# Strassen-type block sums in the output projections of a two-layer LRU and attention kernel, and an output bias added by DMA

## What is computed

```python
# layer 0                                            D_MODEL = D_RNN = 2048, SEQ = 256
return (jax.nn.gelu(gate_br) * rec) @ w_out + b_out      # (256 x 2048) @ (2048 x 2048) + row
# layer 1
return o.reshape(bsz, seq, N_HEADS * V_D) @ w_o          # (256 x 2048) @ (2048 x 2048)
# both layers
h = h + block(rmsnorm(h, norm_mix[layer]))
h = h + swiglu(rmsnorm(h, norm_ffn[layer]))
```

## Time and profile before

| | |
|---|---|
| median of 3 runs | 1996.56 us (1995.83 to 1996.84) |
| the profiled execution: its own time | 1996.43 us |
| its span in the profile | 1994.6 us |
| PE busy | 1974.2 us, 99%, 9907 matmuls |
| DVE busy | 1649.1 us, 83% |
| ACT busy | 1136.6 us, 57% |
| POOL busy | 76.5 us, 4% |
| loads of `lru_w_out`, `w_o` | 16 of 1 MB each |
| `project(0)` | 227.5 to 316 us of the span |
| `project(2)` | 1191 to 1289 us of the span |

### The profile page before, as it was taken

How to read it: one execution, slowest core, us unless ns; L and a number is a source line. 1 busy time by engine, 2 the same in 40 slices (tenths; PEclk the granted TensorE clock), 3 DMA queues, 4 the chain that set the end, 5 groups by cost and what they waited for, 6 DMA issues and landing times.

```text
span 1994.6 us, 26207 instructions
## 1 busy us (share of the span) xinstructions
PE 1974.2 (99%) x9907; PEld 1683.8 (84%) x9907; DVE 1649.1 (83%) x1849; ACT 1136.6 (57%) x1356; POOL 76.5 (4%) x113
## 2 busy tenths in 40 slices
PE   7999999999999999999999999999999999999999
PEld 7999988888888888888898888888888888888887
DVE  6868655788888889999976886468988898899897
ACT  5478445555555556556676664455555555556564
POOL 1140200000000000000001110000000000000000
PEclk9999999999999999999999999999999999999999
DMA  8564663556556565565565435355656556655554
GB/s 278 170 206 158 206 212 115 199 193 202 197 191 209 191 204 194 195 206 192 209 201 169 127 126 185 111 189 192 205 194 205 194 191 208 193 196 203 200 202 168
DMA packets 159488, 378.21 MB, mean 190 GB/s; under 512 B 6154, under 2 KB 10516, under 8 KB 159028
## 3 DMA queue, kind: packets, MB, share of 16 engines
q1 hardware_dynamic: 158960, 376.02, 56.4%
q0 software_dynamic: 272, 1.13, 0.2%
q10 hardware_dynamic: 180, 0.05, 0.0%
HBM read 375.08 MB, written 2.10 MB: 189 GB/s over the span
## 4 chain that ended last, share of the span: by engine, by line
PE 89%; issue 5%; DVE 2%; ACT 1%; DMA 1%; POOL 1%; POOLq 0%; SPq 0%; DVEq 0%; ACTq 0%
PE bank L1731 75%; PE bank L1912 10%; PE bank L1692 2%; PE bank L1724 1%; PE bank L1715 1%; DVE w_lo L1005 0%; POOL stats L1676 0%; DMA h<-in_x 0%; ACT w_hi L555 0%; DMA raw<-in_ffn_w_in 0%; DMA raw<-in_ffn_w_out 0%; PE bank L1894 0%; ACT gtmp L687 0%; ACT w_hi L618 0%; ACT w_lo L621 0%
## 5 line engine op out<-in xcount | busy, mean ns | idle before, releaser
L1731 PE MATMUL bank<-w_hi,act_hi 128*128 128x512 f32 x1840 | 720.2, 391 | 1.7 <-issue 1.5
L1731 PE MATMUL bank<-w_hi,act_lo 128*128 128x512 f32 x1840 | 716.4, 389 | 0.0
L555 ACT ACTIVATE w_hi<-raw 128x2048 fp32r<-128x2048 f32 (+2 forms) x271 | 509.8, 1884 | 331.6 <-DMA raw<-in_ffn_w_in 149.5
L1731 PE MATMUL bank<-raw_lo,act_hi 128*128 128x512 f32 x1584 | 616.4, 389 | 0.0
L1005 DVE TENSOR_TENSOR raw_lo<-raw,w_hi 128x2048 fp32r<-128x2048 f32 x176 | 401.8, 2288 | 112.6 <-ACT w_hi L555 110.5
L1731 PEld LDWEIGHTS bank<-w_hi,act_hi 128*128 128x128 f32 x1840 | 345.5, 188 | 74.9 <-issue 2.6
L1731 PEld LDWEIGHTS bank<-w_hi,act_lo 128*128 128x128 f32 x1840 | 345.4, 188 | 72.1
L1731 PEld LDWEIGHTS bank<-raw_lo,act_hi 128*128 128x128 f32 x1584 | 297.5, 188 | 60.5
L1005 DVE TENSOR_TENSOR w_lo<-raw,w_hi 128x2048 fp32r<-128x2048 f32 (+2 forms) x95 | 211.8, 2240 | 84.3 <-ACT w_hi L555 84.0
L1055 DVE TENSOR_TENSOR raw_lo<-raw,w_hi 128x2048 fp32r<-128x2048 f32 x88 | 201.0, 2284 | 0.0
L618 ACT ACTIVATE w_hi<-raw 128x1024 fp32r<-128x1024 f32 x88 | 93.0, 1057 | 130.0 <-DMA raw<-in_ffn_w_in 107.9
(11 more groups left out here) (230 smaller groups left out, 2440.5 us busy)
## 6 DMA issues: line engine op xcount, KB each, us to landing
raw<-in_ffn_w_in SPq DMA_DIRECT2D x176, 1024.0 KB, 5.3
raw<-in_ffn_w_out SPq DMA_DIRECT2D x88, 1024.0 KB, 4.9
raw<-in_lru_w_in SPq DMA_DIRECT2D x32, 1024.0 KB, 5.4
raw<-in_lru_w_out SPq DMA_DIRECT2D x16, 1024.0 KB, 5.4
raw<-in_w_o SPq DMA_DIRECT2D x16, 1024.0 KB, 5.0
raw<-in_w_ukv SPq DMA_DIRECT2D x8, 1024.0 KB, 5.4
raw<-in_w_uq SPq DMA_DIRECT2D x8, 768.0 KB, 4.5
raw<-in_w_dkv SPq DMA_DIRECT2D x8, 576.0 KB, 4.3
```

What stands on the lines that cost most here:

```text
L555: A.activation(flat_chunk(w_hi, s, size), flat_chunk(raw, s, size), ACT.Copy).then_inc(w_hi_done, 1)
L1731: i = T.matmul(bank[:, :], x_part, w_part, start=first and n == 0, stop=last and n == 2)
```

## The change

In both projections, units 4 and 5 of the first pass and units 1 and 3 of the second (9 and 11 of the 16) become units of seven block products. With them come their activation sums, a `p1_out`, a `shared_add` and a `shared_to_h` in each pass, which stand in iterations 5 and 11. All low parts of the projections' chunks go to `raw_lo`, so all loads from chunk 4 of a projection on, and the first four of the following `up`, wait for `chunk_used`. The second pass has as its own banks those that were shared in the first, and shares the first pass' own: unit 8 waits for the first `shared_add` (`u_done`), unit 9 for the first pass' `results_to_h` (`h_done`). The bias is added to `h` by two DMAs that POOL starts as soon as its last multiply of the gate stage is done.

The core of the diff, in the order SP, ACT, DVE, POOL, PE (the helpers of `two_pass` were split so that `project` can call them too, and numbers of semaphores shifted with them):

```diff
+PROJ_SUMS = ((4, 5), (1, 3))
...
-                    unit(0, u, slice(0, W), u >= 4)
+                    unit(0, u, slice(0, W), True)
...
-                         raw[n % 4].rearrange("p (k f) n -> p k (f n)", k=2), in_place)
+                         raw[n % 4].rearrange("p (k f) n -> p k (f n)", k=2), in_place or n >= 4)
...
+            def p1_out(d, half, n):
+                act.wait_ge(chunk_used, DOWN_C[d] + n + 1)
+                act.wait_ge(h_shared, 2 * d + half)
+                A.activation(gtmp[:, 0, :], shared_banks(d, half)[0][:, :], ACT.Copy).then_inc(p1_done, 1)
...
                         stationary(d, g, wo_slot(g) if d else act_slot(g))
+                    half, v = divmod(n, KT // 2)
+                    if v == PROJ_SUMS[half][-1]:
+                        p1_out(d, half, n)
...
-                    split((DOWN_C[d] + n + 4) // 4, n % 4)
+                    proj_split(d, n + 4)
...
             def project(d):
                 for n in range(KT - 4):
+                    half, v = divmod(n, KT // 2)
+                    if v == PROJ_SUMS[half][-1]:
+                        if half:
+                            dve.wait_ge(h_sq, NB * d + 2)
+                        shared_to_h(d, half)
                     if n in (1, 3) or n == d == 0:
                         g = (n + 3) // 2
                         stationary(g, wo_slot(g) if d else act_slot(g), DOWN_G0[d] + g + 1)
                     if n == KT // 2 - 1:
                         results_to_h(d, 0, KT // 2)
-                    split((DOWN_C[d] + n + 4) // 4, n % 4)
+                    if proj_sum_no(n + 4) is not None:
+                        proj_sums(d, n + 4)
+                    proj_split(d, n + 4)
...
-            pool.wait_ge(y_done, 4)
-            pool.dma_start(bout[:, :], a["lru_b_out"][0:1, :].broadcast_to([P, D])).then_inc(bout_in, 16)
-            pool.wait_ge(bout_in, 16)
             for t in range(NT):
-                i = G.tensor_tensor(h[:, t, :], h[:, t, :], bout[:, :], ALU.add)
-            i.then_inc(bout_added, 1)
+                pool.dma_start(h[:, t, :], a["lru_b_out"][0:1, :].broadcast_to([P, D]),
+                               accum_op=ALU.add).then_inc(bout_added, 16)
...
+                if v == 0 and half:
+                    pe.wait_ge(u_done, U_DONE * (d // 2) + 1)
                 pe.wait_ge(w_lo_done, DOWN_C[d] + n + 1)
+                no = proj_sum_no(n)
+                if no is not None:
+                    pe.wait_ge(g_sum_lo, A_SUMS * (d // 2) + no + 1)
+                    if n == KT // 2 + PROJ_SUMS[1][0]:
+                        pe.wait_ge(h_done, NB * d + 2)
+                    i = sum_unit(s, no % 2, no % 3, k0, result, shared_banks(d, half), v == PROJ_SUMS[half][0],
+                                 v == PROJ_SUMS[half][-1], tiles=DOWN_TILES)
```

More of the change, by code:

```diff
@@ L521, in down_unit_no, with proj_sum_no @@
         def down_unit_no(f, n):
-            return SUMS * f + 3 * S_BLOCKS + down_sum_no(n)
+            return SUMS * f + PROJ_ALL + 3 * S_BLOCKS + down_sum_no(n)
+        def proj_sum_no(n):
+            half, v = divmod(n, KT // 2)
+            return len(PROJ_SUMS[0]) * half + PROJ_SUMS[half].index(v) if v in PROJ_SUMS[half] else None
         def banks_of(odd):
@@ L532, in pass_banks, with shared_banks @@
             return banks if d % 2 else [banks[n] for n in (0, 2, 1, 3)]
+        def shared_banks(d, half):
+            return banks_of((half + d) % 2 == 1)[1]
         def sum_tiles(t, e):
@@ L640, in two_pass @@
                 c0 = DOWN_C[d]
-                def p1_out(n, half):
-                    act.wait_ge(chunk_used, c0 + n + 1)
-                    act.wait_ge(h_shared, 2 * f + half)
-                    A.activation(gtmp[:, 0, :], banks_of(half == 0)[1][0][:, :], ACT.Copy).then_inc(p1_done, 1)
                 for n in range(DOWN_UNITS - 4):
@@ L997, in _, with split @@
             V = nc.vector
-            def split(m, s, of_pair=False, to=w_lo):
+            def split(m, s, of_pair=False, to=None):
                 if isinstance(m, int) and 4 * m + s >= CHUNKS:
                     return
+                if to is None:
+                    n = 4 * m + s if isinstance(m, int) else 0
+                    to = raw_lo if C_LOUT <= n < C_DKV or n >= C_WO else w_lo
                 size = chunk_size(4 * m + s if isinstance(m, int) else s + (C_PAIR if of_pair else 0))
@@ L1089, in down_sums, with activation_sums_lo, proj_sums, proj_split @@
                 V.tensor_tensor(s_raw[:, j, 3, :], a12, s_raw[:, j, 1, :], ALU.add).then_inc(g_sum, 1)
+            def activation_sums_lo(o, j):
+                dve.wait_ge(g_sum_hi, o + 1)
+                V.tensor_tensor(s_lo[:, j, :, :], s_raw[:, j, :, :], s_hi[:, j, :, :].bitcast(F32),
+                                ALU.subtract).then_inc(g_sum_lo, 1)
+            def proj_sums(d, n):
+                no, half, v = proj_sum_no(n), n // (KT // 2), n % (KT // 2)
+                m, s = (DOWN_C[d] + n) // 4, n % 4
+                k0 = 2 * ((v + KT // 4 * half) % (KT // 2)) if d else 2 * v
+                source_ready(dve, d, k0 // 4)
+                dve.wait_ge(chunk_used, 4 * m + s - 3)
+                activation_sums(k0, A_SUMS * (d // 2) + no, no % 3)
+                sums(m, s, SUMS * (d // 2) + no, no % 2, DOWN_TILES)
+            def proj_split(d, n):
+                m, s, no = (DOWN_C[d] + n) // 4, n % 4, proj_sum_no(n)
+                if no is None:
+                    split(m, s)
+                else:
+                    activation_sums_lo(A_SUMS * (d // 2) + no, no % 3)
+                    split_sums(m, s, SUMS * (d // 2) + no, no % 2)
+            def down_sums(f, n):
+                d, g_no = 2 * f + 1, down_sum_no(n)
+                v, o, j = n % PASS_UNITS, A_SUMS * f + PROJ_ALL + g_no, g_no % 3
+                m, s = (DOWN_C[d] + n) // 4, n % 4
+                dve.wait_ge(gT_act, FB * f + v // 2 + 1)
+                dve.wait_ge(chunk_used, 4 * m + s - 3)
+                activation_sums(2 * v, o, j)
                 sums(m, s, down_unit_no(f, n), g_no % 2, DOWN_TILES)
@@ L1109, in results_to_h @@
                 result = pass_banks(d, half)
-                if d % 2:
-                    dve.wait_ge(h_shared, d + half)
-                elif d == 0 and half == 0:
-                    dve.wait_ge(bout_added, 1)
+                dve.wait_ge(h_shared, 2 * d + half + 1)
                 for b in (0, 1):
@@ L1142, in into_next, with shared_to_h @@
                     split((c_next + n) // 4, n, to=w_lo if d == 1 else raw_lo)
+            def shared_to_h(d, half):
+                f = d // 2
+                before = S_BLOCKS + 2 if d % 2 else 0
+                shared_add(shared_banks(d, half), SUM_BLOCKS * f + before + half,
+                           U_DONE * f + (FB + 2 if d % 2 else 0) + half)
+                if d == half == 0:
+                    dve.wait_ge(bout_added, 16 * NT)
+                for t in range(NT):
+                    hb = h[:, t, (2 * half) * W:(2 * half + 1) * W]
+                    V.tensor_tensor(hb, hb, gtmp[:, t, :], ALU.add)
+                for t in range(NT):
+                    hb = h[:, t, (2 * half + 1) * W:(2 * half + 2) * W]
+                    i = V.tensor_tensor(hb, hb, mix[:, t, :], ALU.subtract)
+                i.then_inc(h_shared, 1)
             def project(d):
                 for n in range(KT - 4):
+                    half, v = divmod(n, KT // 2)
+                    if v == PROJ_SUMS[half][-1]:
+                        if half:
+                            dve.wait_ge(h_sq, NB * d + 2)
+                        shared_to_h(d, half)
                     if n in (1, 3) or n == d == 0:
@@ L1756, in last_unit, with sum_unit @@
                 return i
-            def sum_unit(s, e, j, k0, result, shared, first, last, gT_needed, tiles=UP_TILES):
+            def sum_unit(s, e, j, k0, result, shared, first, last, gT_needed=None, tiles=UP_TILES):
                 own = [tuple(buf[s][:, n, :] for buf in (w_hi, raw_lo)) for n in tiles]
@@ L1768, in sum_unit @@
                 product(shared[3], s3, t3, first, last)
-                if first:
+                if first and gT_needed is not None:
                     pe.wait_ge(gT_act, gT_needed)
@@ L1812, in half_units @@
                         pe.wait_ge(w_lo_done, DOWN_C[d] + n + 1)
-                    i = plain_unit(n, tile_of(d, 0, n), pass_banks(d, 0), n == 0, False, tiles=DOWN_TILES, lo=w_lo, halves=(half,))
+                    i = plain_unit(n, tile_of(d, 0, n), pass_banks(d, 0), n == 0, False, tiles=DOWN_TILES, halves=(half,))
                     if half:
```

89 lines of the change are left out of this document (40 added, 49 removed).

## The result

The changed kernel takes **2010.35 us**, the median of 4 runs (2009.52 to 2012.46), against 1996.7 for the kernel before, run beside it: a ratio of 1.0070, 95% interval 1.0058 to 1.0082. It is slower by 13.7 us, within the range of the prediction and 4 us above its value. The profiled execution has a span of 2007.7 us, 13.1 more than before.

What follows compares the result with a forecast made beforehand. PE, busy 99%, sets the time if DVE delivers. Waits 14.8 plus restarts 0.5 less gain 5.44 is +9.9 us: span 2006.3, with 0.13 to the median 2006.4 us; own range 2003 to 2010, wider range 2000 to 2012.5.

Steps and rivals of the forecast that it cites:

- The gain: Both projections: eight units lose three matmuls each, 24 x 0.2268 = 5.44 us saved, 2.72 us per projection.
- The waits: Projections: PE waits for DVE at units 5 and 9, and at unit 4 of project(2), 14.8 us in all.
- Nothing for the bias and for the low parts in the slots: Bias by two accumulating DMAs, and later loads for the next up stage: each costs 0 us.
- Restart after a wait: After each of five PE waits, matmuls don't overlap with earlier ones: 0.1 us each, 0.5 us, bounds 0 and 0.39.
- The clock: Rival, chance 0.10: three PE waits of 3.35 to 5.5 us bring the clock down, 3 x 2.35 = 7 us, 2013.4.
- a cold array: Program start: matmuls 0.21 us apart, later 0.13, read as a possible slow state from 12.2 to 16.9.
- the helpers keep up: Rival, chance 0.10: DVE runs further ahead in the projections, waits shrink to nothing, only the 5.44 us saved is left, 1991.1.
- only unit 9 waits: Rival, chance 0.10: unit 9 waits but unit 5 does not, or the reverse; waits of 7 to 10 us, about 2000.
- two between most: Down stage: two plain units stand between most units of seven products, one at the least; argued against the faster rival.

Runs made afterwards that it cites:

- unit 5 taken away: The changed kernel with units 4, 9 and 11 of seven products, unit 5 plain again: 2001.26 us, ratio 1.0025 to the kernel before.
- the pair moved: The changed kernel with the second pass' units 10 and 11 of seven products in place of 9 and 11: 2004.72 us, ratio 1.0048 to the kernel before.
- the result one chunk earlier: The changed kernel with DVE's four adds of the first pass' result to h ahead of chunk 10's low part: 2004.37 us.
- units 5, 11: The changed kernel with only units 5 and 11 of seven products, one per pass: 1994.78 us, ratio 0.9992 to the kernel before.

## Why the prediction was right, and which term was too small

*The gain.* Right: 9883 matmuls, and the sums above close with 0.2268 us each.

The measured 2010.35 us lies inside the range of 2000 to 2012.5, and 0.35 us above the inner one of 2003 to 2010. The sum behind the value was right in its largest terms and 4 us short in two small ones.

*The waits.* Right, place by place:

| place | predicted | measured |
|---|---|---|
| project(0), unit 5 | 0.7 | 0.71 |
| project(0), unit 9 | 5.5 | 5.57 |
| project(2), unit 4 | 0.6 | 0.62 |
| project(2), unit 5 | 3.35 | 3.09 |
| project(2), unit 9 | 4.65 | 4.37 |
| sum | 14.8 | 14.36 |

DVE's adds end at 281.8 where 281.5 was worked out. The step that carried it, to follow DVE through the pass with durations of the down stage, held to 0.3 us at every place, and two edits (unit 5 taken away, the pair moved) moved the waits as it says.

*Nothing for the bias and for the low parts in the slots.* Right, each measured alone at 0.9998 (0.9989 to 1.0008). The two DMAs did not land like the loads, though: a median of 11.1 us against 5.4. The working's upper bound had been 6.4 us for each, one after the other, and that was too low: they landed 8.0 and 14.2 us after their issue at 139.0 and 139.6. But they ran side by side, the later one was in at about 154, ACT took the chunk of the earlier trace rows at 162.95 against 162.83 before, and `h` itself is needed 110 us later.

*"Restart after a wait ... I take 0.1 each."* Too small: 0.3, within the bounds given (0 to 0.39). For five waits 1.5 us in place of 0.5. The bounds came from the right cause, a matmul without a neighbour to overlap with, and 0.28 us of it are in the rows. The reason for going to the low end, that weights can be loaded ahead, does not touch it.

*The clock, which the sum left at nothing.* This is the step that failed. The rival had three waits x 2.35 = 7 us with a chance of 0.10; two of the three lost 1.86 and 1.49, and the third, of 3.09 us, lost nothing in this execution and 1.5 to 1.6 in two other versions. So its mechanism was there and its size about half of what it said.

Of the two arguments against it, the first ("the waits before are too short to tell") says that the trace of before can't show the price. Such a cost is bounded from both sides and given weight, not set to 0. The second, that the first matmuls of the program are slow for operands just written while 384 GB/s of loads arrive, is answered by other runs. Two versions that are the same program up to there, the result one chunk earlier and units 5, 11, have these windows (from:to, length, busy us of PE and matmuls, granted clock, DMA share, GB/s):

```profile
16.00:17.00 1.00, 1.00 (x7) 1.00 1.06 391
16.00:17.00 1.00, 1.00 (x11) 1.00 1.05 389
```

The same matmuls under the same loads are slow in one and fast in the other. In the first of the two the slow ones go on to 18.0 (line 1984 is the matmul of the input projection):

```profile
17.78 0.42 PE L1984 MATMUL bank<-act_hi,w_hi 128*128 128x256 f32 x1
18.00 0.34 PE L1984 MATMUL bank<-act_lo,w_hi 128*128 128x256 f32 x1
18.18 0.28 PE L1984 MATMUL bank<-act_hi,w_lo 128*128 128x256 f32 x1
```

The shown 1.00, which the prediction held against its own reading, says nothing there: the record of the clock in a trace has no entry for the first microseconds, and the windows print 1.00 where it has none. Its first entry begins at 16.94 in the kernel before, 18.11 and 15.38 in these two, and in all twelve traces (15.38 to 18.35) the steps between matmuls shorten there, within one matmul, from 0.21 us to 0.12 or 0.11, whichever matmul stands at that place. So the reading "a cold array" was right: the program starts at the lower level. Only the length taken from it was too much. From 12.2 to 16.9 are 4.7 us, while PE worked at that level for 4.1 and 3.3 us behind its two long waits, since the clock falls while PE still stands.

The four us between 2006.4 and 2010.35 are these two: 1.0 + 3.35, less 0.4 for waits a little shorter. That the time stayed in the range with a term of 3.35 us put at nothing is owed to the range's width, not to the sum.

*The other rivals.* That the helpers keep up, and that only unit 9 waits, fell with the first view of the profile. The version with units 5 and 11 shows what the first would need: one such unit per pass is absorbed, but for a wait of 0.66 us. (Of the six gaps between such units in a pass of the down stage, three have two plain units and three have one, not "two between most".)

What would gain more stays open. That DVE's sums move to another engine was not tried.

## What to carry to other kernels

When a kernel is bound by one engine at 99%, fewer instructions on it are worth something only if the engine that prepares its operands still has slack at that place. Follow that engine unit by unit, with the durations of the same work elsewhere in the trace, and add whatever else it owes in between. Price a wait of TensorE above its own length: 0.3 us for the restart, and 1.4 to 2.2 us for half clock, which came behind 8 of 21 waits of 1.7 to 3.4 us and behind all ten of 3.96 us and more. Spread the dear units so that none begins before the helper has caught up with the last: of the five sets of units tried here, only the one with a single such unit per pass was not slower. And where a view shows a clock of 1.00, look at the steps between matmuls too: at the program's start they told the clock and the view did not.
